# Neighbourhood attention in a two-layer transformer: two heads at a time in TensorE's halves

## The chip, the cores and the metric

One core of one Trainium2 chip. The time is microseconds of device time for one launch; the profile is one execution taken by the hardware profiler.

## What is computed

A two-layer transformer over 256 latent and 256 context tokens, width 1024. The second layer's mixer is neighbourhood attention, 16 heads of 64. The latent tokens are 4 grid rows of 64; a query sees 16 columns around its own in all 4 rows, with a bias looked up by row and column distance, and all 256 context keys. Cut to the core:

```python
s_nb = jnp.einsum('bqhd,brqwhd->bhqrw', q_r, k_win) * scale + bias
s_ctx = jnp.einsum('bqhd,bkhd->bhqk', q_r, k_ctx) * scale
p = jax.nn.softmax(jnp.concatenate([s_nb.reshape(...), s_ctx], axis=-1), axis=-1)
out = einsum(p_nb, v_win) + einsum(p_ctx, v_ctx)
```

Before it comes the first layer with its gated MLP; after it an output projection, a router and a mixture of 8 experts.

## The kernel before

One hand-scheduled program in stages (`STAGES`, line 42), each engine's part written out in order. `begin(eng, me, stage)` (line 252) makes an engine wait until every other engine has finished the stages ahead of it. The stages around the change are `norm2`, `qkv` (project q, k, v: six weight chunks of 2 MB through a ring of three slots), `natt` (the attention), `out1` (output projection), `norm3`, `route`, `moe`.

**Work items of natt.** `N_ITEMS` (line 238) has 32 items: 16 heads by two tiles of 128 queries. The keys are always all 512 (256 latent, with everything outside the window at -1e30, and 256 context). Per item:

- PE, `scores` (2164): q against all 512 keys into one PSUM bank (2167), contraction over the head's 64 rows only, partitions 0 to 63 or 64 to 127. Then a second matmul (2169) adds the bias into the first 256 columns: stationary is the constant `FLIP`, which turns each 64 queries round and multiplies by 8, because the bias tile comes from HBM with the query order reversed.
- DVE, `largest` (1350): maximum over 512 columns (1353), times -scale (1354). ACT (883): exponential with row sum. DVE, `normalise` (1357): reciprocal (1359), multiply 128x512 in SBUF (1361).
- PE: 4 transposes (1938); ACT copies them to SBUF (896); PE: 4 matmuls with the values (1948), whose 64 output columns go to PSUM partitions 0 to 63 or 64 to 127; DVE, `take_out` (1363): copy to `OC` (1366).

The engines run these as a pipeline written out by hand: in iteration i PE does scores(i), transposes(i-2), values(i-3); ACT exp(i), copy(i-2); DVE largest(i), normalise(i-1), take_out(i-4). Scores use 3 banks, transposes 2, results 2. A float32 matmul shows as two records of the profile, a transpose as one.

**The bias.** SP issues two DMAs per item (525), 64 KB each in 256-byte pieces, into one of 4 tiles of `BM`; the first follow `begin(sp, None, "natt")` (516), the rest wait for the scores of four items back (521). GpSimd adds the window mask `WM` to each tile (688).

**Queues.** SP also loads all weights: the stream loop (489 to 511) waits for a slot to be freed and issues the chunk (503); behind the bias loads come the expert weights (547, 551). In qkv, ACT (746) and GpSimd (587) split the weights of each half chunk in a high and a low part ahead of PE, and ACT (1051) and DVE (1536) move the projections out of PSUM, to the places that `qkv_place` (244) gives. `QB` (line 110, 12 x 512 columns) is free from the end of norm2 until the gate rows of out1.

Of the kernel before, what the change touches and what calls it, by code (L numbers as in the profile page):

```python
# [8 lines left out]
P = 128  # L9
# [24 lines left out]
RING, REGIONS = 3, 7  # L34
GROUP = 448
RING_E, SLOT_E = 8, 8 * GROUP
IDENT, UP, LO, SLO, SUP, LEV5, LEV6, ROT, IOTA, FLIP, SMALL = range(11)
N_CONST = 11
R_C, R_NG, R_CONV, R_QG, R_KVG = 0, 16, 48, 108, 111
WAVES = E + 3  # L40

STAGES = ["prep", "norm0", "win", "tok", "l2", "ga", "mproj", "matt", "sub", "kv", "gdn", "gout", "out0", "norm1", "up",
          "down", "norm2", "qkv", "natt", "out1", "norm3", "route", "moe", "final"]
# [8 lines left out]
def constants():  # L52

    i = np.arange(P)
    m = np.zeros((P, N_CONST, P), np.float32)
    r, c = i[:, None], i[None, :]
    m[:, IDENT] = r == c
    m[:, UP] = r <= c
    m[:, LO] = r >= c
    m[:, SLO] = r > c  # L60
    m[:, SUP] = r < c
    for n, at in ((5, LEV5), (6, LEV6)):
        m[:, at] = (r >> (n + 1) == c >> (n + 1)) & (r >> n > c >> n)
    m[:, SMALL, 0:32] = r % 32 > np.arange(32)[None]
    m[:, SMALL, 32:64] = r % 32 == np.arange(32)[None]
    q = ROPE // 4
    for a in range(q):
        for half in (0, 2 * q):
            m[NOPE + half + q + a, ROT, NOPE + half + a] = -1.0
            m[NOPE + half + a, ROT, NOPE + half + q + a] = 1.0  # L70
    m[:, IOTA] = c

    m[:, FLIP] = ((r // GRID_W == c // GRID_W) & (r % GRID_W == GRID_W - 1 - c % GRID_W)) * float(DH) ** 0.5
    t = np.arange(L)
    inv = np.float32(10000.0) ** (-np.arange(0, ROPE // 2, 2, dtype=np.float32) / np.float32(ROPE // 2))
    ar = (t // GRID_W).astype(np.float32)[:, None] * inv[None]
    ac = (t % GRID_W).astype(np.float32)[:, None] * inv[None]
    ang = np.concatenate([ar, ar, ac, ac], axis=-1)
    rope = np.stack([np.cos(ang).T, np.sin(ang).T], axis=1).astype(np.float32)
    col = GRID_W - 1 - i % GRID_W  # L80
    first = np.clip(col - WIN_C // 2, 0, GRID_W - WIN_C)[:, None]
    key = np.arange(GRID_W)[None]
    window = np.where((key >= first) & (key < first + WIN_C), 0.0, -1e30).astype(np.float32)
    return m.reshape(P, -1), rope, window


def build(nc, A, out):
# [4 lines left out]
    with ctx:  # L92
# [9 lines left out]
        def sem(name):  # L102
            return ctx.enter_context(nc.semaphore(name))
# [98 lines left out]
        QC = cut(KB, L)  # L202
        KC = cut(KB, T)
        VC = cut(NT, D)
        PC = cut(3, T)
        PCT = cut(2, 4, P)
        BM = cut(4, L)
        OC = HB[:, 0:KB * L].rearrange("p (k t) -> p k t", t=L)
        cut = Cut(QB)
        XG = cut(KB, P)  # L210
# [24 lines left out]

        TILE_OF = [[2, 3, 0, 1], [3, 2, 1, 0]]
        M_ITEMS = [(h, t, 4 if t < 2 else 2) for h in range(H_B) for t in range(NT)]
        N_ITEMS = [(h, t, 4) for h in range(H_C) for t in range(2)]

        PS = ctx.enter_context(nc.psum_tensor("PS", [P, 8, 512], f32))  # L240

        done = {e: sem(f"{e}_stage_done") for e in WORKS}

        def qkv_place(i):

            if i < 8:
                return QC[:, i, :], PS[:, i % 4, 0:L]
            if i < 16:
                return KC[:, i - 8, :], PS[:, i % 4, :]
            return VC[:, i % 4, 512 * (i // 20):512 * (i // 20) + 512], PS[:, i % 4, :]  # L250

        def begin(eng, me, stage):

            for e in WORKS:
                n = sum(s in WORKS[e] for s in STAGES[:STAGES.index(stage)])
                if e != me and n:
                    eng.wait_ge(done[e], n)
# [131 lines left out]
        def unit_parts(eng, key):  # L389
# [28 lines left out]
        att_s, att_max, att_p, att_pn, att_tr, att_pt, att_o, att_oe = (sem(n) for n in (  # L418
            "scores_mm", "scores_max", "probs_ready", "probs_normed", "probs_transposed", "probs_t_ready", "pv_mm",
            "pv_evacuated"))  # L420
        bias_in, bias_ok = [sem(f"rpb_in{i}") for i in range(4)], sem("bias_masked")
        l2_sq, l2_ss, l2_sd, l2_r, l2_bc, l2_ok, l2_tr, l2_ev = (sem(n) for n in (
            "l2_squares", "l2_sums", "l2_sd", "l2_rstd", "l2_broadcast", "l2_scaled", "kv_transposed", "kv_tokens"))
# [47 lines left out]
        def _(sp):  # L471
# [10 lines left out]
            def load_constants():  # L482
# [6 lines left out]
                sp.dma_start(GG[:, :], everywhere(A["ev_gdn_norm_g"], P)).then_inc(s_misc, 16)  # L489
                sp.dma_start(RW[:, :, :], A["od_router"][0].rearrange("(k p) n -> p k n", p=P)).then_inc(s_misc, 16)  # L490

            for i, (shape, source, _) in enumerate(stream):
                if i == first["up2"]:
                    sp.wait_ge(bias_zero, 2)
                    load_ada_b(1)
# [17 lines left out]

            begin(sp, None, "natt")
            rpb = A["od_rpb"]
            for j in range(2 * H_C):
                h, qt = j // 2, j % 2
                if j >= 4:  # L520
                    sp.wait_ge(att_s, len(M_ITEMS) + j - 3)
                for r in range(2):
                    at = h * RPB_R * RPB_C + (WIN_R - 1 - (2 * qt + r)) * RPB_C + WIN_C - GRID_W
                    src = bass.AP(tensor=rpb.tensor, offset=at, ap=[[1, GRID_W], [RPB_C, ROWS], [1, GRID_W]])
                    sp.dma_start(BM[64 * r:64 * r + 64, j % 4, :].rearrange("p (a b) -> p a b", a=ROWS),
                                 src).then_inc(bias_in[j % 4], 16)

            wg, wu = (A[n].rearrange("o e (b k p) n -> (o e) b p k n", b=2, p=P) for n in ("od_exp_wg", "od_exp_wu"))
            wd = A["od_exp_wd"].rearrange("o e (j p k) n -> (o e) j p (k n)", p=P, k=7)
# [39 lines left out]
        def _(pool):  # L569
# [110 lines left out]
                     [(f"qkv{c}", h) for c in (4, 5) for h in range(2)])  # L680


            begin(pool, "pool", "natt")
            for j in range(2 * H_C):
                pool.wait_ge(bias_in[j % 4], 32 * (j // 4 + 1))
                v = BM[:, j % 4, :].rearrange("p (a b) -> p a b", a=ROWS)
                m = WM[:, :].rearrange("p (a b) -> p a b", a=1).to_broadcast([P, ROWS, GRID_W])
                pool.tensor_tensor(v, v, m, ALU.add).then_inc(bias_ok, 1)
            pool.wait_ge(bias_ok, 2 * H_C)
            pool.nop().then_inc(done["pool"], 1)  # L690

        @block.scalar
        def _(act):
# [362 lines left out]

            begin(act, "act", "natt")
            act.dma_start(FG, everywhere(A["final_norm_g"], D)).then_inc(s_fg, 16)
            attention(N_ITEMS, len(M_ITEMS), PC, PCT, DH ** -0.5)

            gate_rows("out1", 2, GB, 1)
            squares(2, out_ev, lambda i: 2 * NT + 2 + i + 1, 6)
# [66 lines left out]
        def _(dve):  # L1129
# [250 lines left out]
            def out_of(j):  # L1380
                h, t, _ = M_ITEMS[j]
                return YB[64 * (h % 2):64 * (h % 2) + 64, h // 2, t * P:t * P + P]
# [156 lines left out]

            begin(dve, "dve", "natt")  # L1540

            def out_of(j):
                h, t, _ = N_ITEMS[j]
                return OC[64 * (h % 2):64 * (h % 2) + 64, h // 2, t * P:t * P + P]

            attention(N_ITEMS, len(M_ITEMS), PC, out_of, DH ** -0.5)

            add_out("out1", 2 * NT, 2)
            norm("norm3", 2, 12, 1, 1, fT)
# [160 lines left out]
        def _(pe):  # L1710
# [5 lines left out]
            def ident(n=P):  # L1716
                return CM[0:n, IDENT, 0:n]
# [443 lines left out]

            begin(pe, "pe", "natt")

            def scores(j):
                h, t, n = N_ITEMS[j]
                rs = slice(64 * (h % 2), 64 * (h % 2) + 64)
                mm(PS[:, j % 3, :], QC[rs, h // 2, t * P:t * P + P], KC[rs, h // 2, :], start=True, stop=False)  # L2167
                pe.wait_ge(bias_ok, j + 1)
                return mm(PS[:, j % 3, 0:L], CM[:, FLIP, :], BM[:, j % 4, :], start=False, stop=True)  # L2169

            attention(N_ITEMS, len(M_ITEMS), PC, PCT, scores, lambda h, i, n: VC[:, i, h * DH:h * DH + DH])

            project("out1", 2 * NT, 2, lambda k, t: OC[:, k, t * P:t * P + P])
            norm("norm3", 2, 12, lambda i: X[:, 2 + i, :])
# [142 lines left out]
```

## Time and profile before

| | us |
|---|---|
| median of 3 runs (lowest, highest) | 2281.72 (2277.76, 2283.62) |
| the profiled execution, its own time | 2278.74 |
| its span, first to last instruction | 2276.8 |
| mean granted TensorE clock | 0.931 of full |

The span holds all engine work; some 2 us of the run lie outside it. Engines: PE is TensorE, PEld its weight loads, DVE VectorE, ACT ScalarE, POOL GpSimd, SP the queue that issues DMAs. The granted clock is 1.00 for 2.4 GHz and 0.50 for 1.2 GHz.

### The profile page before, as it was taken

How to read it: one execution, taken by the hardware profiler on the slowest of the kernel's cores; microseconds unless marked ns; L12 is line 12 of the kernel's file. 1: busy time of each engine (PE TensorE's matmuls, PEld its weight loads, DVE VectorE, ACT ScalarE, POOL GpSimd, SP SyncE). 2: the span in 40 equal slices, each digit the busy share in tenths (PEclk: the TensorE clock that was granted, in tenths of full speed). 3: DMA queues.
4: the chain of work that ended last, by engine and by line, in shares of the span. 5: the costliest groups of instructions: out<-in, count | busy, mean ns of one | idle time of the engine just before them, and what ended most of it. 6: DMA issues, size and time to landing. Idle time of an engine off the chain costs nothing.

```text
span 2276.8 us, 24303 instructions
## 1 busy us (share of the span) xinstructions
PE 2000.3 (88%) x9801; PEld 1197.1 (53%) x9802; DVE 624.3 (27%) x1274; ACT 526.5 (23%) x853; POOL 401.7 (18%) x241
## 2 busy tenths in 40 slices
PE   4999778968899998979899698998988899888786
PEld 2787335956677767868665443343433344333332
DVE  3933356644100014450054320110211100111012
ACT  3332224543221221232133110110211110211021
POOL 0431530532233433435221000000000000000000
PEclk8999879979899998989999799999999999999998
DMA  8443000112345451223353679877999978799995
GB/s 313 148 155 119 1 0 1 38 74 74 112 161 208 149 187 72 93 74 111 94 41 25 258 279 415 343 290 262 401 407 418 402 296 301 284 417 407 416 409 223
DMA packets 147117, 482.68 MB, mean 212 GB/s; under 512 B 23268, under 2 KB 48213, under 8 KB 132645
## 3 DMA queue, kind: packets, MB, share of 16 engines
q1 hardware_dynamic: 145984, 477.89, 56.4%
q8 instruction: 114, 1.87, 0.3%
q10 hardware_dynamic: 997, 2.75, 0.3%
q14 instruction: 22, 0.18, 0.0%
HBM read 479.56 MB, written 1.05 MB: 211 GB/s over the span
## 4 chain that ended last, share of the span: by engine, by line
PE 60%; DMA 8%; DVE 4%; issue 2%; ACT 2%; SPq 1%; POOL 0%; DVEq 0%; ACTq 0%; POOLq 0%
PE PS L2239 20%; DMA BIG<-in_od_exp_wu 8%; PE PS L1753 7%; PE PS L1754 7%; PE PS L1755 7%; PE PS L2285 7%; PE PS L2167 2%; PE PS L1948 1%; PE PS L2215 1%; PE PS L2230 1%; PE PS L2087 1%; DVE HB L1190 1%; SPq L547 1%; PE PS L2169 1%; PE PS L1732 1%
## 5 line engine op out<-in xcount | busy, mean ns | idle before, releaser
L2239 PE MATMUL PS<-BIG,QB 128*64 128x448 f32 x2560 | 516.1, 562 | 72.4 <-issue 41.9
L2239 PEld LDWEIGHTS PS<-BIG,QB 128*64 128x64 f32 x2560 | 185.3, 142 | 383.3 <-issue 375.7
L2285 PE MATMUL PS<-BIG,QB 128*64 128x512 f32 x1120 | 245.5, 593 | 1.3 <-DMA BIG<-in_od_exp_wd 0.7
L587 POOL TENSOR_TENSOR BIG_parts<-BIG,QB_parts 128x2048 fp32r<-128x2048 f32 x33 | 152.7, 4627 | 282.8 <-ACT QB_parts L746 282.8
L587 POOL TENSOR_TENSOR BIG_parts<-BIG,BIG_parts 128x2048 fp32r<-128x2048 f32 (+1 forms) x28 | 126.1, 4503 | 248.3 <-ACT BIG_parts L746 248.3
L2285 PEld LDWEIGHTS PS<-BIG,QB 128*64 128x64 f32 x1120 | 89.5, 137 | 151.3 <-issue 148.6
L1754 PE MATMUL PS<-HB_parts,QB_parts 128*128 128x512 f32 x352 | 137.3, 390 | 0.0
L1669 DVE TENSOR_TENSOR HB<-HB,PS 128x512 f32<-128x512 f32 x36 | 24.8, 688 | 380.4 <-PE PS L2215 380.4
L1754 PE MATMUL PS<-BIG_parts,BIG_parts 128*128 128x512 f32 (+1 forms) x336 | 127.4, 379 | 0.0
L1753 PE MATMUL PS<-ZS_parts,BIG_parts 128*128 128x512 f32 (+1 forms) x240 | 92.5, 385 | 10.0 <-DVEq L1200 8.1
L1755 PE MATMUL PS<-BIG_parts 128*128 128x512 f32 (+1 forms) x256 | 96.3, 376 | 0.0
L1753 PE MATMUL PS<-YB_parts,BIG_parts 128*128 128x512 f32 (+1 forms) x240 | 90.5, 377 | 0.0
L1498 DVE TENSOR_TENSOR BIG<-BIG,PS 128x512 f32<-128x512 f32 x22 | 15.1, 688 | 257.3 <-ACT BIG L1015 257.3
L746 ACT ACTIVATE QB_parts<-BIG 128x2048 fp32r<-128x2048 f32 x33 | 63.0, 1910 | 93.5 <-PE PS L1755 89.8
L1754 PE MATMUL PS<-HB_parts,BIG_parts 128*128 128x512 f32 (+1 forms) x224 | 82.5, 368 | 0.0
L1687 DVE TENSOR_TENSOR MOD<-HB,PS 64x448 f32<-64x448 f32 x32 | 19.7, 615 | 226.3 <-ACT HB L1090 226.3
L1094 ACT ACTIVATE QB<-PS 128x896 f32<-128x896 f32 x32 | 29.4, 918 | 221.0 <-PE PS L2230 221.0
L1089 ACT ACTIVATE HB<-PS 64x448 f32<-64x448 f32 x64 | 34.6, 541 | 181.3 <-PE PS L2239 181.3
L1754 PEld LDWEIGHTS PS<-HB_parts,QB_parts 128*128 128x128 f32 x352 | 66.1, 188 | 13.3
L1504 DVE TENSOR_TENSOR BIG_parts<-BIG,BIG_parts 128x1024 fp32r<-128x1024 f32 x11 | 53.1, 4833 | 67.0 <-ACT BIG_parts L1023 67.0
L1687 DVE TENSOR_TENSOR QB<-HB,PS 64x448 f32<-64x448 f32 x32 | 19.7, 615 | 188.0 <-ACT HB L1090 188.0
L1113 ACT ACTIVATE HB<-PS 64x512 f32<-64x512 f32 x20 | 11.8, 592 | 255.1 <-PE PS L2285 255.0
(340 smaller groups left out, 3052.0 us busy)
## 6 DMA issues: line engine op xcount, KB each, us to landing
BIG<-in_od_exp_wg SPq DMA_DIRECT2D x64, 1792.0 KB, 19.0
BIG<-in_od_exp_wu SPq DMA_DIRECT2D x64, 1792.0 KB, 21.2
BIG<-in_od_exp_wd SPq DMA_DIRECT2D x64, 1792.0 KB, 21.1
BIG<-in_ada_w SPq DMA_DIRECT2D x24, 2048.0 KB, 8.1
BIG<-in_od_w_qkv SPq DMA_DIRECT2D x6, 2048.0 KB, 7.9
BIG<-in_ev_ffn_wg SPq DMA_DIRECT2D x11, 1024.0 KB, 8.8
BIG<-in_ev_ffn_wu SPq DMA_DIRECT2D x11, 1024.0 KB, 11.3
BIG<-in_ev_ffn_wd SPq DMA_DIRECT2D x5, 2048.0 KB, 8.8
```

Source lines behind the costliest of these rows:

```text
L587: pool.tensor_tensor(r12(w), w, r12(high), ALU.subtract).then_inc(split_l, 1)
L746: act.activation(r12(high), w, ACT.Copy).then_inc(split_h, 1)
L1089: act.activation(SE[0:64, s % 2, :], PS[64:P, 2 + s % 2, 0:GROUP], ACT.Silu)
L1094: act.activation(HET[:, 7 * p:7 * p + 7, :].rearrange("p a b -> p (a b)"), PS[:, 4:6, :].rearrange("p a b -> p (a b)")[:, 0:7 * P], ACT.Co ...
L1504: dve.tensor_tensor(r12(v), v, r12(HHIGH[:, j % 2]), ALU.subtract).then_inc(h2_low, 1)
L1687: dve.tensor_tensor(to[64:P, :], SE[0:64, s % 2, :], PS[0:64, 2 + s % 2, 0:GROUP], ALU.mult)
L1753: mm(to, wl, mh, start=(k == 0), stop=False)
L1754: mm(to, wh, ml, start=False, stop=False)
L1755: last = mm(to, wh, mh, start=False, stop=(k == n_k - 1))
L2167: mm(PS[:, j % 3, :], QC[rs, h // 2, t * P:t * P + P], KC[rs, h // 2, :], start=True, stop=False)
L2239: last = mm(PS[at:at + 64, bank, 0:GROUP], XG[:, 4 * part + k, r0:r0 + 64], wgu[u][:, k, GROUP * c:GROUP * c + GROUP], start=(part + k == ...
L2285: last = mm(PS[64 * n:64 * n + 64, bank, :], HET[:, 7 * q + k, c0:c0 + 64], slot_e[:, a, :], start=(q + k == 0), stop=(q == NPAIR - 1 and ...
```

## The change

Items become 16 pairs of heads (`N_PAIRS`). The scores of both heads are issued together, one in array rows 0 to 63, one in 64 to 127, each to its own bank, two banks per pair, double-buffered. The `FLIP` matmul goes. Instead q is written in turned order when it leaves PSUM in qkv (`turned`, step -1), VectorE adds the bias to the scores in PSUM with one `scalar_tensor_tensor` over both heads, one reduction finds both maxima, and the result is turned back in `take_out`, one copy of 128x128 per pair. The value matmuls of the two heads alternate between output columns 0 to 63 and 64 to 127 of one bank. The second head's probabilities are multiplied by GpSimd. `BM` moves to `QB` with 12 pair tiles: SP loads 12 pairs, 16 DMAs each time, ahead of qkv chunks 3, 4 and 5, after a wait for `begin(sp, None, "qkv")`; GpSimd masks all 12 behind its last weight split; the last 4 pairs follow in natt. The copy of the transposes has one bank per head. All arithmetic stays float32, and the number of bias bytes is the same.

```diff
+NBIAS = 12
...
@@ -202,9 +201,9 @@
         QC = cut(KB, L)
         KC = cut(KB, T)
         VC = cut(NT, D)
-        PC = cut(3, T)
-        PCT = cut(2, 4, P)
-        BM = cut(4, L)
+        PC = cut(6, T)
+        PCT = cut(4, 4, P)
+        BM = QB[:, :].rearrange("p (i a k) -> p i a k", i=NBIAS, a=2)
...
-        N_ITEMS = [(h, t, 4) for h in range(H_C) for t in range(2)]
+        N_PAIRS = [(h, t) for h in range(H_C // 2) for t in range(2)]
+        NP = len(N_PAIRS)
...
+        def turned(ap):
+            (stride, parts), (step, n) = [list(d) for d in ap.ap]
+            return bass.AP(tensor=ap.tensor, offset=ap.offset + (GRID_W - 1) * step,
+                           ap=[[stride, parts], [GRID_W * step, n // GRID_W], [-step, GRID_W]])
         def qkv_place(i):
             if i < 8:
-                return QC[:, i, :], PS[:, i % 4, 0:L]
+                return turned(QC[:, i, :]), PS[:, i % 4, 0:L].rearrange("p (a q) -> p a q", q=GRID_W)
...
+            rpb = A["od_rpb"]
+            def load_bias(i):
+                hp, qt = N_PAIRS[i]
+                if i >= NBIAS:
+                    sp.wait_ge(att_max, len(M_ITEMS) + i - NBIAS + 1)
+                if i >= 4:
+                    sp.wait_ge(bias_in[i % 4], 64 * (i // 4))
+                for a in range(2):
+                    for r in range(2):
+                        at = (2 * hp + a) * RPB_R * RPB_C + (WIN_R - 1 - (2 * qt + r)) * RPB_C + WIN_C - GRID_W
+                        src = bass.AP(tensor=rpb.tensor, offset=at, ap=[[1, GRID_W], [RPB_C, ROWS], [1, GRID_W]])
+                        sp.dma_start(BM[64 * r:64 * r + 64, i % NBIAS, a, :].rearrange("p (r k) -> p r k", r=ROWS),
+                                     src).then_inc(bias_in[i % 4], 16)
             for i, (shape, source, _) in enumerate(stream):
+                if first["qkv"] + 3 <= i < first["qkv"] + 6:
+                    if i == first["qkv"] + 3:
+                        begin(sp, None, "qkv")
+                    for k in range(4):
+                        load_bias(4 * (i - first["qkv"] - 3) + k)
...
-            begin(sp, None, "natt")
-            rpb = A["od_rpb"]
-            for j in range(2 * H_C):
-                h, qt = j // 2, j % 2
-                if j >= 4:
-                    sp.wait_ge(att_s, len(M_ITEMS) + j - 3)
-                for r in range(2):
-                    at = h * RPB_R * RPB_C + (WIN_R - 1 - (2 * qt + r)) * RPB_C + WIN_C - GRID_W
-                    src = bass.AP(tensor=rpb.tensor, offset=at, ap=[[1, GRID_W], [RPB_C, ROWS], [1, GRID_W]])
-                    sp.dma_start(BM[64 * r:64 * r + 64, j % 4, :].rearrange("p (a b) -> p a b", a=ROWS),
-                                 src).then_inc(bias_in[j % 4], 16)
+            for i in range(NBIAS, NP):
+                load_bias(i)
...
+            def window(i):
+                pool.wait_ge(bias_in[i % 4], 64 * (i // 4 + 1))
+                v = BM[:, i % NBIAS, :, :].rearrange("p a (r k) -> p (a r) k", r=ROWS)
+                m = WM[:, :].rearrange("p (a b) -> p a b", a=1).to_broadcast([P, 2 * ROWS, GRID_W])
+                pool.tensor_tensor(v, v, m, ALU.add).then_inc(bias_ok, 1)
+            for i in range(NBIAS):
+                window(i)
             begin(pool, "pool", "natt")
-            for j in range(2 * H_C):
-                pool.wait_ge(bias_in[j % 4], 32 * (j // 4 + 1))
-                v = BM[:, j % 4, :].rearrange("p (a b) -> p a b", a=ROWS)
-                m = WM[:, :].rearrange("p (a b) -> p a b", a=1).to_broadcast([P, ROWS, GRID_W])
-                pool.tensor_tensor(v, v, m, ALU.add).then_inc(bias_ok, 1)
-            pool.wait_ge(bias_ok, 2 * H_C)
+            for i in range(NP):
+                pool.wait_ge(att_r, i + 1)
+                v = PC[:, 2 * (i % 3) + 1, :]
+                pool.tensor_scalar(v, v, RT[:, 25 + 2 * (i % 4):26 + 2 * (i % 4)], None, ALU.mult).then_inc(att_pb, 1)
+                if i + NBIAS < NP:
+                    window(i + NBIAS)
+            pool.wait_ge(bias_ok, NP)
+            pool.wait_ge(att_pb, NP)
             pool.nop().then_inc(done["pool"], 1)
         @block.scalar
...
             act.dma_start(FG, everywhere(A["final_norm_g"], D)).then_inc(s_fg, 16)
-            attention(N_ITEMS, len(M_ITEMS), PC, PCT, DH ** -0.5)
+            base, scale = len(M_ITEMS), DH ** -0.5
+            for i in range(NP + 2):
+                if i < NP:
+                    act.wait_ge(att_max, base + i + 1)
+                    for a in range(2):
+                        if i >= 3:
+                            act.wait_ge(att_tr, base + 2 * (i - 3) + a + 1)
+                        at = 2 * (i % 4) + a
+                        act.activation(PC[:, 2 * (i % 3) + a, :], PS[:, 2 * (i % 2) + a, :], ACT.Exp,
+                                       bias=RT[:, at:at + 1], scale=scale,
+                                       accum_out=RT[:, 16 + at:17 + at]).then_inc(att_p, 1)
+                j = i - 2
+                if j >= 0:
+                    if j >= 2:
+                        act.wait_ge(att_o, base + j - 1)
+                    for a in range(2):
+                        act.wait_ge(att_tr, base + 2 * j + a + 1)
+                        act.activation(PCT[:, 2 * (j % 2) + a, :, :],
+                                       PS[:, 4 + a, :].rearrange("p (a b) -> p a b", a=4), ACT.Copy).then_inc(att_pt, 1)
+            act.wait_ge(att_pt, base + 2 * NP)
...
-            def out_of(j):
-                h, t, _ = N_ITEMS[j]
-                return OC[64 * (h % 2):64 * (h % 2) + 64, h // 2, t * P:t * P + P]
-            attention(N_ITEMS, len(M_ITEMS), PC, out_of, DH ** -0.5)
+            base, scale = len(M_ITEMS), DH ** -0.5
+            def largest(i):
+                v = PS[:, 2 * (i % 2):2 * (i % 2) + 2, :]
+                at = 2 * (i % 4)
+                dve.wait_ge(att_s, base + i + 1)
+                dve.wait_ge(bias_ok, i + 1)
+                seq(dve.scalar_tensor_tensor(v[:, :, 0:L], BM[:, i % NBIAS, :, :], 1.0 / scale, v[:, :, 0:L], ALU.mult,
+                                             ALU.add))
+                seq(dve.tensor_reduce(RT[:, 8 + at:10 + at], v, AX.X, ALU.max))
+                dve.tensor_scalar(RT[:, at:at + 2], RT[:, 8 + at:10 + at], -scale, None, ALU.mult).then_inc(att_max, 1)
+            def normalise(i):
+                at = 2 * (i % 4)
+                dve.wait_ge(att_p, base + 2 * i + 1)
+                seq(dve.reciprocal(RT[:, 24 + at:25 + at], RT[:, 16 + at:17 + at]))
+                v = PC[:, 2 * (i % 3), :]
+                dve.tensor_scalar(v, v, RT[:, 24 + at:25 + at], None, ALU.mult).then_inc(att_pn, 1)
+                dve.wait_ge(att_p, base + 2 * i + 2)
+                dve.reciprocal(RT[:, 25 + at:26 + at], RT[:, 17 + at:18 + at]).then_inc(att_r, 1)
+            def take_out(i):
+                h, t = N_PAIRS[i]
+                dve.wait_ge(att_o, base + i + 1)
+                dve.tensor_copy(turned(OC[:, h, t * P:t * P + P]),
+                                PS[:, 6 + i % 2, 0:P].rearrange("p (a q) -> p a q", q=GRID_W)).then_inc(att_oe, 1)
+            for i in range(NP + 4):
+                if i < NP:
+                    largest(i)
+                if 0 <= i - 1 < NP:
+                    normalise(i - 1)
+                if i - 4 >= 0:
+                    take_out(i - 4)
+            dve.wait_ge(att_oe, base + NP)
+            dve.nop().then_inc(done["dve"], 1)
...
-            def scores(j):
-                h, t, n = N_ITEMS[j]
-                rs = slice(64 * (h % 2), 64 * (h % 2) + 64)
-                mm(PS[:, j % 3, :], QC[rs, h // 2, t * P:t * P + P], KC[rs, h // 2, :], start=True, stop=False)
-                pe.wait_ge(bias_ok, j + 1)
-                return mm(PS[:, j % 3, 0:L], CM[:, FLIP, :], BM[:, j % 4, :], start=False, stop=True)
-            attention(N_ITEMS, len(M_ITEMS), PC, PCT, scores, lambda h, i, n: VC[:, i, h * DH:h * DH + DH])
+            base = len(M_ITEMS)
+            for i in range(NP + 3):
+                if i < NP:
+                    h, t = N_PAIRS[i]
+                    if i >= 2:
+                        pe.wait_ge(att_p, base + 2 * (i - 2) + 2)
+                    for a in range(2):
+                        rs = slice(64 * a, 64 * a + 64)
+                        last = mm(PS[:, 2 * (i % 2) + a, :], QC[rs, h, t * P:t * P + P], KC[rs, h, :], start=True,
+                                  stop=True)
+                    last.then_inc(att_s, 1)
+                j = i - 2
+                if 0 <= j < NP:
+                    for a in range(2):
+                        pe.wait_ge(*((att_pb, j + 1) if a else (att_pn, base + j + 1)))
+                        if j:
+                            pe.wait_ge(att_pt, base + 2 * (j - 1) + a + 1)
+                        for c in range(4):
+                            last = pe.transpose(PS[:, 4 + a, c * P:c * P + P], PC[:, 2 * (j % 3) + a, c * P:c * P + P],
+                                                ident())
+                        last.then_inc(att_tr, 1)
+                j = i - 3
+                if j >= 0:
+                    h, t = N_PAIRS[j]
+                    pe.wait_ge(att_pt, base + 2 * j + 2)
+                    if j >= 2:
+                        pe.wait_ge(att_oe, base + j - 1)
+                    for c in range(4):
+                        for a in range(2):
+                            last = mm(PS[64 * a:64 * a + 64, 6 + j % 2, 0:P],
+                                      VC[:, c, (2 * h + a) * DH:(2 * h + a) * DH + DH],
+                                      PCT[:, 2 * (j % 2) + a, c, :], start=(c == 0), stop=(c == 3))
+                    last.then_inc(att_o, 1)
+            pe.wait_ge(att_o, base + NP)
+            end()
```

## Rows read from the trace of the kernel before

**Rows 1.** The page: the chain that ended last, shares of the span by engine.

```profile
PE 60%; DMA 8%; DVE 4%; issue 2%; ACT 2%; SPq 1%; POOL 0%; DVEq 0%; ACTq 0%; POOLq 0%
```

**Rows 2.** Windows: stretch, length, busy PE, PEld, DVE, ACT, POOL, granted clock, DMA share, GB/s.

```profile
1126.40:1133.80 7.40, 1.09 (x2) 0.29 (x2) 0.00 (x0) 1.28 (x1) 0.72 (x1) 0.64 0.60 100
1133.80:1148.60 14.80, 14.78 (x31) 7.34 (x32) 5.61 (x14) 4.09 (x10) 4.35 (x6) 0.50 0.55 52
1148.60:1241.20 92.60, 91.99 (x480) 57.36 (x478) 48.49 (x146) 36.64 (x86) 18.16 (x25) 1.00 0.48 36
398.00:402.00 4.00, 2.29 (x15) 1.42 (x13) 0.84 (x3) 3.48 (x8) 0.82 (x1) 0.99 0.00 2
1241.20:1270.70 29.50, 29.42 (x68) 12.84 (x68) 4.15 (x7) 2.23 (x4) 0.00 (x0) 1.00 0.34 125
```

**Rows 3.** The chain of waits in natt, start and length: at half clock, at full.

```profile
1142.21 2.00 PE PS L2167 x2
...
1145.36 0.85 PE PS L1938 x4
1146.21 1.90 PE PS L1948 x8
...
1154.83 1.05 PE PS L2167 x2
1155.88 0.63 PE PS L2169 x2
1156.51 0.44 PE PS L1938 x4
1156.95 1.02 PE PS L1948 x8
```

**Rows 4.** Groups by form, natt alone: busy us, mean ns, idle before and releaser.

```profile
L2167 PE MATMUL PS<-BIG 64*128 64x512 f32 x64 | 39.2, 694 | 0.9 <-DVEq L1538 0.9
...
L1353 DVE TENSOR_REDUCE RT<-PS 128x1 f32<-128x512 f32 x32 | 22.1, 692 | 55.5 <-PE PS L2169 55.5
L883 ACT ACTIVATE BIG<-PS,RT 128x512 f32<-128x512 f32 x32 | 22.0, 687 | 69.4 <-DVE RT L1354 69.4
...
L896 ACT ACTIVATE BIG<-PS 128x512 f32<-128x512 f32 x32 | 18.8, 588 | 1.2 <-PE PS L1938 1.1
L1361 DVE TENSOR_SCALAR BIG<-BIG,RT 128x512 f32<-128x512 f32 x32 | 16.7, 523 | 1.1
...
L1366 DVE COPY HB<-PS 64x128 f32<-64x128 f32 x32 | 9.1, 285 | 2.9 <-PE PS L1948 2.4
...
L1354 DVE TENSOR_SCALAR RT<-RT 128x1 f32<-128x1 f32 x32 | 4.9, 154 | 1.1
```

**Rows 5.** Timeline, expert stage: column halves in turn.

```profile
1328.44 3.98 PE L2239 MATMUL PS<-BIG,QB 128*64 128x448 f32 x20
```

**Rows 6.** The page: VectorE adding an SBUF tile to a PSUM bank.

```profile
L1498 DVE TENSOR_TENSOR BIG<-BIG,PS 128x512 f32<-128x512 f32 x22 | 15.1, 688 | 257.3 <-ACT BIG L1015 257.3
```

**Rows 7.** Groups by form, whole run, VectorE: the 256-wide reduction.

```profile
L1353 DVE TENSOR_REDUCE RT<-PS 128x1 f32<-128x256 f32 x16 | 6.7, 420 | 3.1 <-PE PS L1958 2.8
```

**Rows 8.** Groups by form, whole run, GpSimd on 512 columns.

```profile
L638 POOL TENSOR_TENSOR BIG<-BIG,CM 128x512 f32<-128x512 f32 x16 | 20.0, 1274 | 11.6 <-ACTq L923 7.5 <-PE PS L1980 4.0
```

**Rows 9.** Line 525, the bias loads, as issued by SP: shortest, median, longest ns.

```profile
L525 SPq DMA_DIRECT2D BIG<-in_od_rpb x64: 595/617/949, 1126.6 to 1223.0; - x64
```

**Rows 10.** DMA queues from 1126 to 1241 us: packets, MB, share of 16 engines.

```profile
q1 hardware_dynamic: 17408, 4.20, 48.1%
```

**Rows 11.** Timeline of PE: the first matmul of qkv.

```profile
1010.43 0.55 PE L1753 MATMUL PS<-ZS_parts,BIG_parts 128*128 128x256 f32 x1 [8.11 <-DVEq L1200]
```

**Rows 12.** Timeline of the SP queue: qkv chunks 3, 4 and 5.

```profile
1024.58 36.17 SPq L503 DMA_DIRECT2D BIG<-in_od_w_qkv  x3
```

**Rows 13.** Timeline of ScalarE: it splits the first half of qkv chunk 3.

```profile
1049.57 1.92 ACT L746 ACTIVATE BIG_parts<-BIG 128x2048 fp32r<-128x2048 f32 x1 [4.90 <-PE PS L1755]
```

**Rows 14.** Timeline of GpSimd: its last work ahead of natt.

```profile
1105.97 4.59 POOL L587 TENSOR_TENSOR BIG_parts<-BIG,BIG_parts 128x2048 fp32r<-128x2048 f32 x1 [6.27 <-ACT BIG_parts L746]
```

More of the change, by code:

```diff
@@ L36 @@
 RING_E, SLOT_E = 8, 8 * GROUP
-IDENT, UP, LO, SLO, SUP, LEV5, LEV6, ROT, IOTA, FLIP, SMALL = range(11)
-N_CONST = 11
+IDENT, UP, LO, SLO, SUP, LEV5, LEV6, ROT, IOTA, SMALL = range(10)
+N_CONST = 10
 R_C, R_NG, R_CONV, R_QG, R_KVG = 0, 16, 48, 108, 111
 WAVES = E + 3
+NBIAS = 12
 STAGES = ["prep", "norm0", "win", "tok", "l2", "ga", "mproj", "matt", "sub", "kv", "gdn", "gout", "out0", "norm1", "up",
@@ L71, in constants @@
     m[:, IOTA] = c
-    m[:, FLIP] = ((r // GRID_W == c // GRID_W) & (r % GRID_W == GRID_W - 1 - c % GRID_W)) * float(DH) ** 0.5
     t = np.arange(L)
@@ L420, in build @@
             "pv_evacuated"))
+        att_r, att_pb = sem("second_reciprocal"), sem("second_probs_normed")
         bias_in, bias_ok = [sem(f"rpb_in{i}") for i in range(4)], sem("bias_masked")
@@ L1058, in _ @@
             act.dma_start(FG, everywhere(A["final_norm_g"], D)).then_inc(s_fg, 16)
-            attention(N_ITEMS, len(M_ITEMS), PC, PCT, DH ** -0.5)
+            base, scale = len(M_ITEMS), DH ** -0.5
[18 more added lines that the diff above has]
+            act.wait_ge(att_pt, base + 2 * NP)
+            act.nop().then_inc(done["act"], 1)
             gate_rows("out1", 2, GB, 1)
```

## The prediction

> **What bounds the kernel now.** I read the page first: the chain that ended last is mostly PE [rows 1]. So what PE does in natt counts, and what follows only shifts with it: the expert weights are queued behind natt and out1 and the expert stage is entered through the router, so I take every microsecond won or lost in natt one to one.
>
> The windows cut natt in three [rows 2]. From 1126.4 to 1133.8 PE has two records, then waits for the first bias tile. From 1133.8 to 1148.6 it is busy at clock 0.50, the 1.2 GHz level. From 1148.6 to 1241.2 it is busy at 1.00. Sum 7.4 + 14.8 + 92.6 = 114.8 us.
>
> The chain gives the item [rows 3]: at full clock scores 1.05, bias 0.63, transposes 0.44, values 1.02, together 3.14 us; 32 items are 100.5 us. PE never waits there: VectorE waits 55.5 us in all for PE and ScalarE 69.4 us for VectorE [rows 4]. PE is the bound of this stage.
>
> **Removed.** The bias matmul, 32 x 0.63 = 20.2 us. The wait for the first bias, about 6 us: the tile is now resident.
>
> **PE per pair.** Transposes: 2 x 0.44 = 0.88. Scores: four records; in series 2 x 1.05 = 2.10. With halves that run together, the first head's second record and the second head's first share a slot, three slots of four: 1.58. Values: 16 records, in series 2.04; in turn between column halves 9 slots of 16: 1.15. That column halves do run together is in the expert stage: 20 records of 448 columns take 3.98 us, 0.20 each [rows 5]; one such record alone would be 448/512 of the scores' 0.525, or 0.46. No row shows two row halves together; I carry the column rows over. Bounds for the scores: 1.05 and 2.10; for the values 1.02 and 2.04. Sum 1.58 + 0.88 + 1.15 = 3.61 us, in series 5.02.
>
> On switching, the Trainium skill (TensorEngine Tiling (Array Packing), Key Properties) says that a change of tiling mode drains TensorE. By that rule a pair has as many switches as one item has now, so part of each 1.05 would be paid once per pair and 1.58 would be an upper value, the saving 1 or 2 us larger; no run here separates a drain from other gaps.
>
> **VectorE per pair.** Add with bias, 512 columns of PSUM and SBUF: 0.69, from the nearest row of that kind [rows 6]; upper end the 1024-column price below. Reduction over 1024: 256 columns take 0.420 [rows 7] and 512 take 0.692 [rows 4], so 0.272 more for 256, and 0.692 + 2 x 0.272 = 1.24; upper end two of today's, 1.38. Scaling 0.15, two reciprocals 0.30 (I price one as the small scaling), multiply 0.52, copy out 0.29, now on 128 partitions in turned order; the turn may cost nothing or double it. With gaps about 3.3 us, below the period found next, so the copy's price stays covered.
>
> **ScalarE** 2 x 0.69 + 2 x 0.59 = 2.6 us [rows 4]. **GpSimd** multiplies 512 columns: 1.27 from a two-input operation of this size [rows 8]; ends 0.5 (what VectorE needs) and 2.5. It hides behind VectorE's next add and reduction, with some 0.6 us to spare ahead of the second head's transposes; at 2.5 it would add about 0.3 us per pair.
>
> **The new loop.** The written-out order makes a ring over two pairs, longer than any engine's own work: scores(i), then add, reduction and scaling, then exp of both heads, then on ScalarE behind them the copies of pair i-2, then on PE the second head's transposes of i-1, the values of i-2, and scores(i+2). Lengths: 1.58 + 0.17 (a record ends 0.694 after its start in a slot of 0.525 [rows 4]) + 2.16 (0.69 + 1.24 + 0.15 and two gaps) + 1.46 (exps and reading the sum) + 1.18 + 0.44 + 1.15 + 0.16 (four hand-overs) = 8.3 us. Per pair 4.15 us. Every wait in the change but GpSimd's lies on this ring; behind PE's wait for the second head's copy stand the values and the next scores.
>
> **Start and end.** 15 periods are 62.3 us. The last pair then runs alone: 1.75 + 2.16 + 1.46 + 0.17 (reciprocal) + 1.27 (GpSimd) + 0.44 + 0.17 + 0.59 + 1.15 + 0.20 + 0.29 = 9.7. The first interval is some 1 us short, as scores(1) waits for nothing. Total 71 us at full clock.
>
> PE stands still for some 2.5 us after the first two scores, and today the clock fell after the wait and stayed at 0.50 for 14.8 us [rows 2]. At half clock a pair costs PE 1.5 x 2.00 + 2 x 0.85 + 9/16 x 2 x 1.90 = 6.84 us [rows 3]. So 14.8 us hold 2.2 pairs instead of 3.6: 1.4 x 4.15 = 5.8; the first pairs are slack anyway, I take 5. **natt: 76 us**, 38.8 saved.
>
> **What is moved.** SP: three sets of 16 bias loads ahead of qkv chunks 3, 4, 5, behind a wait for norm2. A load takes SP 0.617 us [rows 9], a set 9.9. The queue's share over natt is 48.1% of some 115 us [rows 10], 55 us for 64 loads: 0.86 each, 13.8 a set. qkv begins at 1010.43 [rows 11] and chunk 3 is issued today at 1024.58, when its slot is free [rows 12]. The first set is issued by 1020.3 and through by some 1026; chunk 3 then lands by about 1036 and is first touched at 1049.57 [rows 13]. The next chunks follow each about 11 to 22 us later with the same 13.8 us ahead of them, so I price this at nothing; the cover is about 13 us per chunk, and if it were gone a set would cost up to its 13.8. The out1 weights behind chunk 5 and the expert weights behind pairs 12 to 15 wait for slots or for the end of natt anyway. GpSimd: 12 window adds at 1.27 behind its last split, which ends at 1105.97 + 4.59 = 1110.6 [rows 14]: done by 1126, as natt starts, while its first multiply is due some 7 us later. Turned q: eight evacuations in qkv, off PE's path; double price would be hidden too.
>
> **The sum.** The profiled execution took 2278.74 us (span 2276.8 and 2 around it). 2278.7 - 38.8 = 2239.9. The median shown lies 3.0 us above this execution: **2243 us**.
>
> **Rivals.** A, the forecast: 2234 (no fall of the clock, ring at 3.9) to 2250 (a dearer add or GpSimd, row halves in series: ring 8.8, +4 us). Chance 0.68.
>
> B, the halves do not run together and the change buys less than it says: PE is the bound at 5.02. 15 x 5.02 + 10.6 + 5 = 91 us, 24 saved: 2258. For it: no row with row halves together, and column records of only 128 columns whose weight load may not hide in half a slot. Against it: [rows 5]. Chance 0.15.
>
> C, weights of qkv late behind the bias sets: one set's 13.8 us uncovered gives 2257. Against: the cover above. 0.05. D, something gains more (below 2234): 0.02.
>
> E, the clock stays at 1.2 GHz through natt, because PE now waits in every pair. PE then needs 6.84 a pair: 16 x 6.84 + 8 = 117 us, 2 more than today: 2284. Where out1 also starts at half clock for as long as natt did, 14.8 us of its 29.5 hold half the work, +7.4: 2291, the case on the **slower side**. It decides from 6.6 us a pair. For it: the fall at 1133.8. Against: in gdn PE was busy 2.29 of 4 us at 0.99 [rows 2], looser than the 3.61 of 4.15 here; and at half clock the PE sum, 6.84, passes the ring, so PE no longer waits, and from that state it rose today at 1148.6. 0.05 for no gain and 0.05 for slower. The Trainium skill (TensorE: Matmul & The Clock Gate, "A second HAM failure mode: psum-queue depth-cycling") says that small waits between groups of matmuls can make the clock swing between its levels; by that rule this case would be the likely one. The gdn row speaks against it.
>
> **How the numbers follow.** 0.3% (7 us) is about what a measurement of this kernel can tell from no change. Faster by more: A, B, C, D: 0.90. Same: 0.05. Slower: 0.05. The range takes in A and B with their ends: 2232 to 2262; outside lie E and the edges of A, B and C.
>
> **What would show it.** No L2169 and no wait for a bias load in natt; natt from about 1126 to 1202; a period of 4.1 to 4.2 us; in the chain PE, VectorE and ScalarE in turn where PE alone stood; add 0.69, reduction 1.24; clock 0.50 only at the start; out1 and all behind it as long as before. Wrong would be a period near 5 with PE alone in the chain (B), a clock of 0.50 in the middle of natt (E), PE waiting for weights in qkv (C), GpSimd's multiply over 2 us.

## The result and the profile after

| | before | changed |
|---|---|---|
| median of the runs | 2281.56 | 2208.13 (2205.11 to 2211.08) |
| profiled execution, span | 2276.8 | 2205.6 |
| ratio | | 0.9678 (0.9663 to 0.9692) |

The change saves 73 us where 39 were forecast. The direction was right, the size was not: 2208 lies below the range of 2232 to 2262.

Where the 71 us between the two spans lie is read by cutting both traces at the same stage borders. The windows of the changed kernel, columns as in [rows 2]; the last stretch is the expert stage:

```profile
1125.50:1133.00 7.50, 4.43 (x16) 1.75 (x16) 5.39 (x10) 4.18 (x9) 1.06 (x1) 0.86 0.36 82
1133.00:1140.00 7.00, 3.01 (x14) 1.44 (x12) 5.65 (x12) 4.36 (x11) 2.73 (x3) 0.90 0.74 95
1140.00:1147.00 7.00, 6.14 (x48) 4.26 (x48) 1.74 (x2) 0.60 (x1) 4.81 (x4) 0.76 0.36 43
1147.00:1196.10 49.10, 40.48 (x378) 26.18 (x372) 35.51 (x90) 31.26 (x76) 21.55 (x14) 1.00 0.00 1
1196.20:1225.70 29.50, 29.42 (x68) 12.84 (x68) 4.16 (x7) 2.23 (x4) 0.00 (x0) 1.00 0.33 125
1270.40:2205.60 935.20, 858.03 (x4248) 350.40 (x4248) 142.88 (x268) 137.65 (x210) 0.00 (x0) 0.96 0.91 362
```

and the expert stage of the kernel before:

```profile
1315.70:2276.80 961.10, 860.02 (x4248) 348.50 (x4248) 142.85 (x268) 137.64 (x210) 0.00 (x0) 0.95 0.89 354
```

The attention stage natt runs from the first scores at 1125.5 to the last copy out at 1196.1, 70.6 us instead of 114.8: 44.2 saved. out1 takes the same 29.5 us at clock 1.00 as before. From the start of out1 to the first expert matmul it is 74.2 us against 74.5. The expert stage, which the change does not touch, takes 935.2 us instead of 961.1: 25.9 us less. With the 0.9 us by which natt begins earlier, that is the whole.

The page of the changed kernel, with the queue that brings instructions:

```profile
span 2205.6 us, 24098 instructions
...
q8 instruction: 50, 0.82, 0.1%
...
PE 57%; DMA 10%; DVE 5%; SPq 3%; ACT 2%; issue 1%; POOL 1%; DVEq 0%; ACTq 0%
```

and the kernel before for that queue, with PE's largest group, whose last column says what ended PE's idle time:

```profile
q8 instruction: 114, 1.87, 0.3%
...
L2239 PE MATMUL PS<-BIG,QB 128*64 128x448 f32 x2560 | 516.1, 562 | 72.4 <-issue 41.9
```

The same group of the changed kernel:

```profile
L2347 PE MATMUL PS<-BIG,QB 128*64 128x448 f32 x2560 | 515.4, 562 | 48.7 <-DMA BIG<-in_od_exp_wu 40.5
```

The queue's packets fell from 114 to 50; in the expert stage itself they fell from 70 to 6. In PE's waits 41.9 us of "issue", time in which PE waited for nothing that the profile names, are gone. PE's waits for weights (`exp_wu`) grew from 19.9 to 40.5 us: PE now reaches weights that are still on their way. The 41.9 us are five waits of 8.0 to 8.7 us, all at the same place, between the last matmul of one pass of the expert loop and the first of the next; the loop has eight passes, so seven returns to its head, and at the other two PE waited some 5.3 us for weights, as it does after the change. One of the five in the timeline of PE, kernel before:

```profile
1564.45 6.60 PE L2285 MATMUL PS<-BIG,QB 128*64 128x512 f32 x29
1579.01 2.51 PE L2239 MATMUL PS<-BIG,QB 128*64 128x448 f32 x6 [7.96 <-issue]
```

In natt the chain has changed hands, as forecast: PE, VectorE and ScalarE take turns. One round of two pairs, start and length:

```profile
1160.60 1.12 PE PS L2263 x8
1161.71 1.02 PE PS L2274 x16
1162.74 1.08 PE PS L2253 x4
...
1163.84 0.71 DVE PS L1599
...
1164.58 1.23 DVE RT L1601
...
1165.83 0.18 DVE RT L1602
...
1166.04 0.03 ACT BIG L1097
...
1166.18 0.44 issue
1166.62 0.86 ACT BIG L1097 x3
1167.48 0.50 ACT BIG L1106
1167.98 0.14 issue
1168.12 1.12 PE PS L2263 x8
```

From one L2263 group to the next it is 7.52 us, so 3.76 per pair.

### The profile page after: what moved, and what is told of

Its sections match the earlier page's. It is cut to its first block, busy times and chain, and to the rows that moved or that the text cites. A ratio compares the mean times of both kernels' runs of the same rounds, so it can differ in the third digit from the quotient of the medians.

```text
span 2205.6 us, 24098 instructions
## 1 busy us (share of the span) xinstructions
PE 1943.3 (88%) x9737; PEld 1166.9 (53%) x9738; DVE 616.8 (28%) x1226; ACT 524.9 (24%) x853; POOL 423.5 (19%) x241
## 3 DMA queue, kind: packets, MB, share of 16 engines
HBM read 479.49 MB, written 1.05 MB: 218 GB/s over the span
## 4 chain that ended last, share of the span: by engine, by line
PE 57%; DMA 10%; DVE 5%; SPq 3%; ACT 2%; issue 1%; POOL 1%; DVEq 0%; ACTq 0%
PE PS L2347 19%; DMA BIG<-in_od_exp_wu 8%; PE PS L1834 8%; PE PS L1835 8%; PE PS L1836 7%; PE PS L2393 6%; SPq L566 2%; PE PS L2323 1%; PE PS L2168 1%; DMA BIG<-in_od_exp_wd 1%; DVE HB L1240 1%; PE PS L2338 1%; PE PS L1813 1%; PE PS L2314 1%; PE PS L2155 1%
## 5 line engine op out<-in xcount | busy, mean ns | idle before, releaser
L2347 PE MATMUL PS<-BIG,QB 128*64 128x448 f32 x2560 | 515.4, 562 | 48.7 <-DMA BIG<-in_od_exp_wu 40.5
## 6 DMA issues: line engine op xcount, KB each, us to landing
BIG<-in_od_exp_wg SPq DMA_DIRECT2D x64, 1792.0 KB, 19.9
```

What stands on the lines that cost most here:

```text
L2347: last = mm(PS[at:at + 64, bank, 0:GROUP], XG[:, 4 * part + k, r0:r0 + 64], wgu[u][:, k, GROUP * c:GROUP * c + GROUP], start=(part + k == ...
```

## The experiments

Two theories for the expert stage. **P**, for place: the loop's code lies differently over the blocks in which instructions are fetched, because natt has fewer PE instructions ahead of it, and is no longer fetched again on each pass. **Q**: the stage gained through what the change does (its earlier end, the order of loads, the clock). For natt: **R**, the ring of the prediction sets the period.

**1. Moving the code alone.** Empty instructions at the head of PE's program, where PE waits for its first loads, move everything behind them:

```diff
+            for _ in range(112):        # 144 in the second run
+                pe.nop().then_inc(shift, 1)
             pe.wait_ge(s_rows, 96)
```

> The kernel before, with 112 empty PE instructions at the head of PE's program, where PE waits for its first loads: the expert loop's code begins as far into a block of 256 instructions as it does in the changed kernel. Theory P (the expert loop lost 26 us because its code had come to lie over one block fewer and is no longer fetched again each wave): instruction packets of the expert stage fall from 70 to under 10, expert stage 961 to about 935 us, total about 2256 us, 25 faster than before. Rival Q (the 26 us come from the attention stage ending earlier, or from weights or clock): nothing changes in the expert stage, total 2282 us, or some us more for the empty instructions.

Measured: 2250.92 us, ratio to before 0.9869 (0.9837 to 0.9901). 51 instruction packets, expert stage 935.0 us. From its page:

```profile
q8 instruction: 51, 0.84, 0.2%
...
L2242 PE MATMUL PS<-BIG,QB 128*64 128x448 f32 x2560 | 513.1, 560 | 47.8 <-DMA BIG<-in_od_exp_wu 33.5
```

> The changed kernel with 144 empty PE instructions at the head of PE's program: the expert loop's code lies again as in the kernel before, everything else as in the changed kernel. Theory P: the fetches come back (about 70 packets in the expert stage), the expert stage is 961 us again, total about 2234 us, which leaves the attention stage's 44 us alone. Rival Q: 2208 us, no change.

Measured: 2234.49 us, 26 more than the changed kernel; ratio to before 0.9802 (0.9783 to 0.982). 114 packets, expert stage 961.0 us. From its page:

```profile
q8 instruction: 114, 1.87, 0.3%
...
L2350 PE MATMUL PS<-BIG,QB 128*64 128x448 f32 x2560 | 515.5, 562 | 73.0 <-issue 42.6
```

Both ways the same switch: 961 us with 114 packets, 935 us with 50 or 51. P holds and Q falls: the kernel before gets the gain with nothing of the change in it, and the change loses it with nothing taken out. The total of the first run fell by 30 us where 25 were expected; its four executions lie 14 us apart, and the 26 us of the expert stage are what the profile shows.

> The changed kernel with 112 empty PE instructions at the head. The expert loop is 1687 instructions long by the built program, 6.6 blocks of 256, and begins 14 instructions into a block; shifted by 112 it begins at 126 and ends 29 instructions into an eighth block. Theory P: the fetches are back, about 114 instruction packets in all and some 26 us more (2234). If the border lies elsewhere (the program has a preamble that is not in the count) it stays at 50 packets and 2208.

> The changed kernel with 80 empty PE instructions at the head: the expert loop begins 94 instructions into a block and ends within the seventh (94 + 1687 = 1781 of 1792). Theory P with the border where the count of the built program puts it: no fetches come back, about 50 instruction packets, 2208 us, as against 114 packets and 2237 us with 112. If the border lies earlier, the fetches are back here too.

Measured, one execution each: with 112, 114 packets, expert stage 965.0 us, total 2237.18. With 80, 68 packets, 948.5 us, total 2220.24, which neither side of its expectation had. From the two pages, 112 first:

```profile
q8 instruction: 114, 1.87, 0.4%
...
q8 instruction: 68, 1.11, 0.2%
```

With 80 the border is not a clean step, and the trace shows in what way. The 18 packets more than in the changed kernel come in two groups of nine, from 1519 to 1602 us and from 1884 to 1968 us. These are the returns that follow the two long passes of the loop, in which the `more` branches are taken (165 us each, where the others take some 94 to 107). After the other five returns nothing was fetched. So the loop is not fetched again in part on every pass, but as fully as elsewhere on two returns of seven. Why only there stays open.

The packets tell more than the form of the waits. With 112 there were the same 114 packets, but "issue" had ten waits of at most 3.7 us, 18.7 in all, and the waits for `exp_wu` were 42.3 us; the stage was as slow all the same.

The Trainium skill (Runtime: NRT & Kernel Launch, Instruction fetch mechanics) says that TensorE has a memory of 128 KiB for instructions, refilled in blocks of 16 KiB or 256 instructions, and that a taken branch to a place outside the window that is held waits for a fetch. The packets agree with the block: 1.87 MB in 114 is 16.4 KB each. The same section says that nothing in the fetch gains from locality. There the measurement differs: in the changed kernel the eight passes of the expert stage brought 6 packets in all, so the loop stayed resident. The 128 KiB would be eight blocks, an estimate from the page's figures. By the count of the built program the loop is 1687 instructions or 6.6 blocks long; it stayed resident where it touches seven blocks (before with 112, and the changed kernel) and was fetched again where it touches eight (before, and after with 112 and 144): 64 packets more over the seven returns to its head, about nine each, one more than the loop touches. With 80 it touches seven by this count and was fetched on two returns, so the rule by blocks is not the whole.

**2. Do the halves run together?**

```diff
-                        rs = slice(64 * a, 64 * a + 64)
+                        rs = slice(0, 64)
```

> The changed kernel, with both heads' scores taken from array rows 0 to 63 (the second head's scores are those of the first, so this run leaves out half of the scores). If row halves run together in full, the four records of a pair go from 1.08 to about 2.1 us; PE's own work per pair becomes 1.12 + 1.02 + 2.1 = 4.2 and the period goes from 3.76 to about 4.3 us, the stage by +9 us, total about 2217. If the four records only look short because of something else, they stay at 1.08 us.

Measured: the four records take 1.93 us instead of 1.08, in the chain:

```profile
1161.63 1.93 PE PS L2254 x4
```

natt is 76.5 us long, 5.9 more and not 9: the period rose from 3.76 to 4.18 us, about as expected, but a longer wait of PE near the start shrank by 1.5. The total is 2211.11, only 3 more and 6 less than expected; in this one execution the expert stage came out 1.3 us shorter and the stages between natt and it 1.2. So row halves do run together, and wholly: 1.08 us for both heads is about what one head took before, 1.05 [rows 3].

```diff
-                    for c in range(4):
-                        for a in range(2):
+                    for a in range(2):
+                        for c in range(4):
```

> The changed kernel with the value matmuls of one head after those of the other, in their own column halves, not in turn. If turn and turn about is what lets the column halves run together, the 16 records go from 1.02 to nearly 2.04 us, the period from 3.76 to about 4.25, total about 2216 us. If the halves overlap whatever the order, or if other work covers it, 1.02 us and 2208 us.

Measured, in one execution: 1.51 us instead of 1.02, halfway between the two forecasts:

```profile
1159.73 1.51 PE PS L2274 x16
```

natt is 74.6 us, a round of two pairs 8.0 instead of 7.52, total 2211.12. Taking turns matters, by half of what full series would cost.

**3. The start of natt.** GpSimd in the changed kernel, timeline:

```profile
1109.48 14.99 POOL L707 TENSOR_TENSOR QB<-QB,WM 128x512 f32<-128x512 f32 x12
1131.94 1.60 POOL L715 TENSOR_SCALAR BIG<-BIG,RT 128x512 f32<-128x512 f32 x1 [7.47 <-DVE RT L1611]
1137.81 1.26 POOL L707 TENSOR_TENSOR QB<-QB,WM 128x512 f32<-128x512 f32 x1 [4.27 <-DMA QB<-in_od_rpb]
1139.05 1.75 POOL L715 TENSOR_SCALAR BIG<-BIG,RT 128x512 f32<-128x512 f32 x1
```

The 12 masks are early, as forecast. But the multiply of pair 1 stands behind the mask of pair 12, whose bias load SP only issues after the first maximum, at 1129.0, and which lands at 1137.7. The multiply starts at 1139.05, 7.1 us after the first.

```diff
-                if i + NBIAS < NP:
-                    window(i + NBIAS)
+                if 5 <= i < 5 + NP - NBIAS:
+                    window(i - 5 + NBIAS)
```

> The changed kernel with GpSimd's masks of pairs 12 to 15 put behind its multiplies 5 to 8, not behind 0 to 3. Theory W (the second multiply stands in GpSimd's order behind the mask of pair 12, and that waits for a bias load which SP only issues after the first maximum, 1129.0 to 1137.7 us): the gap of some 5.5 us ahead of the second multiply goes, the attention stage falls from 70.8 to about 65 us, total about 2202. Rival: the first pairs are slack anyway, PE waits there for VectorE, and no more than 1 or 2 us come.

Measured: 2197.27 us, ratio to before 0.9638 (0.9624 to 0.9651); natt 65.3 us, 5.3 less. The first two multiplies now stand 3.4 us apart:

```profile
1129.51 1.60 POOL L715 TENSOR_SCALAR BIG<-BIG,RT 128x512 f32<-128x512 f32 x1 [7.48 <-DVE RT L1611]
1132.88 1.58 POOL L715 TENSOR_SCALAR BIG<-BIG,RT 128x512 f32<-128x512 f32 x1 [1.76 <-DVE RT L1611]
```

The total fell by twice as much, 10.9 us. Of the 12.4 us between the two profiled spans, 5.3 lie in natt; 3.7 lie in the expert stage, 2.4 ahead of natt and 0.9 between the two, which this edit does not touch. That is the scatter of single executions: in the changed kernel and its six variants without empty instructions natt began anywhere from 1123.1 to 1128.2 us and the expert stage took 931.5 to 935.3, with no edit there. So the length of natt is the number to compare from here on.

**4. The ring.** ScalarE copies pair i-2 ahead of the exponentials of pair i:

```diff
+                j = i - 2
+                if j >= 0: (the two copies)
                 if i < NP: (the two exponentials)
-                j = i - 2
-                if j >= 0: (the two copies)
```

> The changed kernel with ScalarE's two copies of pair i-2 ahead of the two exponentials of pair i. Theory R (the period is a ring over two pairs in which the copies stand between the exponentials and the transposes): the ring is cut and the period falls from 3.76 us; it falls little, to about 3.68, if the next ring is that of GpSimd's multiply of 1.6 us (second reciprocal, multiply, transposes, copies, exponential), total 2 us less; to about 3.4, total 6 us less, if nothing else binds. Rival (an engine is the bound): no change at all.

Measured: 2203.3 us, ratio 0.9664 (0.9648 to 0.9679), period 3.66 us, natt 69.4, 1.2 less. The small gain in the period, as the expectation had it if GpSimd's multiply binds next; the total fell by 4.8 us, of which natt explains 1.2.

> The changed kernel with the late masks, the copies first, and VectorE computing both reciprocals ahead of its own multiply, so that GpSimd starts some 0.5 us sooner. If both rings are as described, VectorE's own work of about 3.4 us per pair becomes the bound: period 3.4 us, stage about 60 us, total about 2197 us, 11 less than the changed kernel. If GpSimd's multiply is not what binds next, the period stays where copies first left it.

```diff
-                dve.wait_ge(att_p, base + 2 * i + 1)
+                dve.wait_ge(att_p, base + 2 * i + 2)
+                dve.reciprocal(RT[:, 25 + at:26 + at], RT[:, 17 + at:18 + at]).then_inc(att_r, 1)
                 seq(dve.reciprocal(RT[:, 24 + at:25 + at], RT[:, 16 + at:17 + at]))
                 v = PC[:, 2 * (i % 3), :]
                 dve.tensor_scalar(v, v, RT[:, 24 + at:25 + at], None, ALU.mult).then_inc(att_pn, 1)
-                dve.wait_ge(att_p, base + 2 * i + 2)
-                dve.reciprocal(RT[:, 25 + at:26 + at], RT[:, 17 + at:18 + at]).then_inc(att_r, 1)
```

Measured: 2195.71 us, ratio 0.9631 (0.9617 to 0.9646), the fastest of the study, though its interval overlaps that of the late masks alone; natt 61.2 us, 4.1 less than with the late masks alone, period 3.50. The expectation had VectorE's own work as the next bound, at 3.4. The chain shows another engine:

```profile
1165.16 0.07 DVE RT L1607
...
1165.32 1.84 POOL BIG L715
...
1167.20 0.66 PE PS L2262 x4
1167.86 1.02 PE PS L2273 x16
1168.88 1.08 PE PS L2252 x4
...
1169.99 0.70 DVE PS L1599
...
1170.72 1.24 DVE RT L1601
...
1171.97 0.17 DVE RT L1602
1172.14 0.07 DVE RT L1607
```

GpSimd's multiply is now on it, and takes 1.84 us instead of 1.57. It now starts together with VectorE's own multiply of 0.49 us; that this is what lengthens it no run shows by itself. The next run is again the changed kernel, with GpSimd's multiply given back to VectorE:

```diff
-                pool.wait_ge(att_r, i + 1)
-                pool.tensor_scalar(v, v, RT[...], None, ALU.mult).then_inc(att_pb, 1)
...
+                dve.tensor_scalar(v, v, RT[...], None, ALU.mult).then_inc(att_pb, 1)
```

> The changed kernel with the second head's multiply undone to VectorE; GpSimd keeps the masks. Theory R (the ring over two pairs sets the period, and neither VectorE's nor GpSimd's multiply lies on it): the period stays at 3.76 us although VectorE now has some 3.8 us of its own work per pair, or rises by 0.1 at most; and no multiply stands behind the mask of pair 12 any more, so the stage loses the 5.3 us that the late masks gave: total about 2200 us. Rival (VectorE is what binds, GpSimd's help is what made the gain): period 4.2 us or more, total 2210 or above.

Measured: 2203.38 us, ratio 0.9659 (0.9632 to 0.9686), natt 66.3 us. In the timeline of PE two pairs take 7.51 us from scores to scores, as in the changed kernel:

```profile
1161.06 1.13 PE L2252 MATMUL PS<-BIG 64*128 64x512 f32 x4
...
1164.77 1.13 PE L2252 MATMUL PS<-BIG 64*128 64x512 f32 x4
...
1168.57 1.13 PE L2252 MATMUL PS<-BIG 64*128 64x512 f32 x4
```

So R holds: in the changed kernel neither VectorE nor GpSimd binds. Handing the multiply to GpSimd brought nothing in steady running, and with the masks where they stand it cost 4.3 us at the start. Whether it pays once the copies are moved was not run: no kernel here has the copies first and both multiplies on VectorE.

## Why the prediction was wrong

**The step that failed** is in its first paragraph: "what follows only shifts with it", and "I take every microsecond won or lost in natt one to one". The expert stage did not shift, it shrank by 25.9 us. The removed and added instructions were priced by the time that they take on PE, and not as code that lies ahead of a loop; the term for the stages behind natt was put at nothing, and it measured 26 us (experiment 1). By the count of the built programs natt has 144 PE instructions fewer, so the loop starts 14 instead of 158 instructions into a block of 256. Nothing in the prediction looked at the row of the instruction queue or at the 41.9 us of "issue" in PE's largest group, and no rival had the tail change length; the one that came true, D ("something gains more", chance 0.02), names no mechanism. With natt at its measured 70.6 and the tail fixed the sum would have been 2278.7 - 44.2 + 3.0 = 2237.5, inside the range, and the changed kernel with 144 empty instructions measured 2234.5.

**In natt** the mechanism was right and terms were off:

| term | forecast | measured |
|---|---|---|
| scores of a pair, with the lag of the last record | 1.58 + 0.17 | 1.08 + 0.02 |
| values of a pair | 1.15 | 1.02 |
| add, reduction, scaling | 2.16 | 2.17 |
| exponentials | 1.46 | 1.44 |
| copies and transposes on the ring | 1.18 + 0.44 | 0.50 + 0.14 + 1.12 |
| ring of two pairs | 8.3 | 7.52 |
| all beside 15 periods | 8.7 + 5 | 14.2 |
| natt | 76 | 70.6 |

The scores are the mis-sized term: 0.65 of the 0.8 us by which the ring was too long. The picture of slots, in which a head's second record overlaps only the other head's first, is wrong for rows and for columns: four records cost two, 16 cost eight. The lower bound given, 1.05, was the right value. The path of the ring was not quite the one forecast either: PE takes it over after the first copy and then does the transposes of both heads, 1.76 us in all, where two copies and the second head's transposes, 1.62, were added up. VectorE's prices, carried over from rows of other widths, were right:

```profile
L715 POOL TENSOR_SCALAR BIG<-BIG,RT 128x512 f32<-128x512 f32 x11 | 17.4, 1585 | 24.7 <-DVE RT L1611 24.7
...
L1601 DVE TENSOR_REDUCE RT<-PS 128x2 f32<-128x1024 f32 x12 | 14.7, 1224 | 0.4
...
L1599 DVE SCALAR_TENSOR_TENSOR PS<-QB,PS 128x512 f32<-128x512 f32 x12 | 8.4, 696 | 13.1 <-PE PS L2253 13.0
```

GpSimd's multiply took 1.585 us on average where 1.27 was carried over from a two-input operation; at the forecast slack of 0.6 it hid.

**The start.** The 5 us for a clock at the lower level came out by luck, for another reason. The granted clock averaged 0.86, 0.90 and 0.76 in the stretches up to 1147, so low clock was there in parts only; what delayed PE was the multiply behind the mask of pair 12. With the late masks of experiment 3 natt is 65.3 us, which leaves 8.9 beside 15 periods of 3.76: the 8.7 that the forecast had without any fall of the clock. "Every wait in the change but GpSimd's lies on this ring" passed over just that one: a wait was named without what stands behind it.

**Rivals.** B (halves in series) is refuted: 1.08 us for the scores of a pair, and 1.93 when both heads use the same rows. C (weights of qkv late) did not come: the chunk loads were issued at 1023.6, 1039.0 and 1059.4, and natt began 1 us earlier than before. E (a clock at the lower level through natt) did not come: from 1147 on the granted clock was 1.00, with PE busy 40.5 of 49.1 us and waiting in every pair. The rule on small waits between groups of matmuls, by which E would have been the likely case, did not show here.

## What to carry to other kernels

When instructions are added or removed ahead of a long loop on an engine, compare the packets of the instruction queue before and after, and look for "issue" waits where the loop begins again. The code's place was worth 26 us here beside the change's own 44, and some empty instructions ahead of the loop told the two apart. A change's own effect is measured only with the loop in the same place. In a hand-written pipeline, find the ring of waits before the busiest engine, and for each new wait ask what stands behind it in the same engine's order.

## What the runs showed of the hardware

- A loop of some 1690 PE instructions lost 26 us of 961 over its eight passes by its place alone (experiment 1), with 70 instruction packets in its stage instead of 6; the waits at its head were up to 8.7 us long.
- Two float32 matmuls of 64 contraction rows each, on the two row halves and into two banks, took 1.08 us together, one alone 1.05 [rows 3], and both on the same half 1.93.
- The value matmuls of two heads on the two column halves took 1.02 us in turn and 1.51 one head after the other; those of one head alone took 1.02 [rows 3].
- GpSimd multiplied 128x512 by a per-partition scalar in 1.57 us, and in 1.84 us in the run in which VectorE's multiply of 128x512 in SBUF began with it.
- A turned write (step -1) showed no price: the copy of 128x128 out of PSUM took 0.272 us, one of 64x128 before 0.285 [rows 4]. No forward copy of 128x128 was run beside it.
